# State space stage of a decoder step: gate and group norm placed in the next group's projection, one K = 2048 output product at the end

## What is computed

```python
xbc_c, conv_new = causal_conv(xbc, conv_state, p['conv_w'], p['conv_b'])     # width 4, then SiLU
xs, Bm, Cm = jnp.split(xbc_c, [D_INNER, D_INNER + SSD_GROUPS * D_STATE], axis=-1)
y, h_new = ssd_scan(xs, dt, A, Bm, Cm, ssm_state)                             # chunks of 128
y = y + p['d_skip'][:, None] * xs
y = y.reshape(b, T, D_INNER) * jax.nn.silu(z)
yg = y.reshape(b, T, SSD_GROUPS, D_INNER // SSD_GROUPS)
yg = yg * lax.rsqrt(jnp.mean(yg * yg, axis=-1, keepdims=True) + EPS)
y = yg.reshape(b, T, D_INNER) * p['norm_ssd']
...
merged = sigmoid(gate_a) * (att @ p['w_attn_out']) + sigmoid(gate_s) * (ssd_y @ p['w_ssd_out'])
```

## Time and profile before

| what | us |
|---|---|
| median of the runs (4490.77 to 4492.65) | 4491.07 |
| the profiled execution | 4487.59 |
| its span, first to last instruction | 4485.8 |
| PE busy in it | 4092.7 (91%) |
| VectorE busy | 1838.2 (41%) |
| ScalarE busy | 725.8 (16%) |
| POOL busy | 223.2 (5%) |
| mean granted TensorE clock | 0.942 of full speed |

### The profile page before, as it was taken

How to read it: one execution, slowest core, us unless ns; L and a number is a source line. 1 busy time by engine, 2 the same in 40 slices (tenths; PEclk the granted TensorE clock), 3 DMA queues, 4 the chain that set the end, 5 groups by cost and what they waited for, 6 DMA issues and landing times. The chain is left out here.

```text
span 4485.8 us, 48370 instructions
## 1 busy us (share of the span) xinstructions
PE 4092.7 (91%) x17960; PEld 2927.2 (65%) x17960; DVE 1838.2 (41%) x3624; ACT 725.8 (16%) x1421; POOL 223.2 (5%) x224
## 2 busy tenths in 40 slices
PE   7999999989977978988988978899988989999997
PEld 5888776656655555665655645566656678888664
DVE  4222220010035676586586575257861143333001
ACT  2000000010021220211311300145611010000000
POOL 0000000000000020010100201200000100000000
PEclk9999999999957989999999988899998999999999
DMA  4121221114132101101001011320022111111111
GB/s 171 76 112 76 94 96 64 45 70 169 71 78 64 36 22 57 38 16 57 33 21 57 28 32 56 100 71 19 6 82 96 65 50 47 38 47 42 69 39 57
DMA packets 98898, 277.21 MB, mean 62 GB/s; under 512 B 18473, under 2 KB 54321, under 8 KB 87073
## 3 DMA queue, kind: packets, MB, share of 16 engines
q1 hardware_dynamic: 80464, 239.13, 15.5%
q0 software_dynamic: 3200, 21.11, 1.3%
q10 hardware_dynamic: 15072, 14.82, 1.1%
HBM read 228.18 MB, written 47.00 MB: 61 GB/s over the span
## 5 line engine op out<-in xcount | busy, mean ns | idle before, releaser
L1648 PE MATMUL banks<-h,arena 128*128 128x344 f32 x1920 | 586.6, 465 | 30.9 <-DMA arena<-in_w_ssd 30.9
L472 PE MATMUL f_ps<-f_a,f_w 128*128 128x344 f32 x2112 | 611.2, 452 | 1.9 <-issue 1.9
L472 PEld LDWEIGHTS f_ps<-f_a,f_w 128*128 128x128 f32 x2112 | 401.1, 190 | 211.3 <-issue 2.3
L1648 PEld LDWEIGHTS banks<-h,arena 128*128 128x128 f32 x1920 | 368.7, 195 | 232.9 <-DMA arena<-in_w_ssd 32.7
L363 PE MATMUL f_ps<-h,f_w 128*128 128x258 f32 x1408 | 327.7, 386 | 13.0 <-ACT h L209 12.1
L363 PE MATMUL f_ps<-room 128*128 128x258 f32 x1408 | 328.3, 393 | 2.5 <-issue 1.8
L363 PE MATMUL f_ps<-h,room 128*128 128x258 f32 x1408 | 320.9, 381 | 1.1 <-DVE f_u L633 1.0
L363 PEld LDWEIGHTS f_ps<-h,f_w 128*128 128x128 f32 x1408 | 269.7, 192 | 64.5 <-issue 23.6
L363 PEld LDWEIGHTS f_ps<-room 128*128 128x128 f32 x1408 | 275.1, 196 | 45.8 <-issue 2.7
L363 PEld LDWEIGHTS f_ps<-h,room 128*128 128x128 f32 x1408 | 266.9, 190 | 41.0 <-DVE f_u L633 1.9
L707 PE MATMUL banks<-y,arena 128*128 128x344 f32 x768 | 239.2, 474 | 38.2 <-DVE y L2058 30.1
(11 more groups left out here) (380 smaller groups left out, 4866.4 us busy)
## 6 DMA issues: line engine op xcount, KB each, us to landing
f_wa<-in_w_ada SPq DMA_DIRECT2D x28, 1024.0 KB
f_w<-in_w_f1i SPq DMA_DIRECT2D x22, 1024.0 KB, 4.7
f_w<-in_w_f2i SPq DMA_DIRECT2D x22, 1024.0 KB, 4.7
arena<-in_w_ssd SPq DMA_DIRECT2D x40, 512.0 KB, 3.6
f_w<-in_w_f1o SPq DMA_DIRECT2D x16, 704.0 KB, 4.1
f_w<-in_w_f2o SPq DMA_DIRECT2D x16, 704.0 KB, 4.1
room<-in_x SPq DMA_DIRECT2D x16, 516.0 KB, 7.7
scr_x<-room SPq DMA_DIRECT2D x16, 516.0 KB, 5.2
```

The lines of the kernel that those rows point to most:

```text
L472: m = nc.tensor.matmul(ps[n][:, q, 0:NC], wo[:, hf, k], a[:, hf * OK + k, n * NC:(n + 1) * NC], start=hf == 0 and k == 0, stop=hf == 1 and ...
L1648: m = nc.tensor.matmul(ps[q][:, c, 0:NC], w[:, q, k], h[:, k, c * NC:(c + 1) * NC], start=k == 0, stop=k == KT - 1)
```

## The change

The loop over g becomes four copies in the code. ssd_out is run once, behind the last scan.

Gate, squares, sums, root and scaling of group g - 1 stand in the projection of group g, for g of 1 to 3: the gate opens VectorE's list; ScalarE's squares stand ahead of its first copies; POOL adds the four squares into one tile (the first is written there); PE sums that tile over the channels with one product for each chunk of 344, behind its third, fourth and fifth chunk; ScalarE's roots stand among the copies of the second tile; VectorE scales behind probe 0. SP stores the finished four tiles (2064 KB) to a scratch in HBM ahead of the sixth weight tile.

H moves from y to room, where S was accumulated; the wait on kept leaves the scan and stands on SP ahead of the load of H. Squares, their sum and the root lie in room as well. The probes get their own tile (above) instead of cv. The counts stand behind chunks 2, 7, 10, 12, 15, 16, 17 and 18. Six halves of top rounds stand in a projection in place of eight; the other 40 stand in the last stage.

The last stage gates group 3 itself, loads the other twelve tiles and multiplies 16 K tiles with each of eight weight tiles (1024 KB each, in xc's memory). Of the first weight tile the twelve old K tiles come first, with the sums behind each chunk, then group 3's four. ScalarE copies each product into S. S is no longer zeroed, and nothing is added into it.

```diff
@@ time_steps
-            nc.gpsimd.memset(S[:], 0.0).then_inc(zeroed, 1)
-            pool.wait_ge(zeroed, UP + 1)
@@ new helpers
+def gate_group(dve, nc, g, xc, zs, y, dskip, skip, gated):
+    for t in range(GT):
+        nc.vector.scalar_tensor_tensor(out=y[:, t], in0=xc[:, t], scalar=dskip[:, g * GT + t:g * GT + t + 1], in1=y[:, t],
+                                       op0=ALU.mult, op1=ALU.add).then_inc(skip, 1)
+        dve.wait_ge(skip, UP + t + 1)
+        nc.vector.tensor_tensor(y[:, t], y[:, t], zs[:, t], ALU.mult).then_inc(gated, 1)
+def add_group(pool, nc, acc, sq, squared, pooled):
+    for t in range(1, GT):
+        pool.wait_ge(squared, UP + t + 1)
...
+        nc.gpsimd.tensor_tensor(acc[:], acc[:], sq[:, t % 2], ALU.add).then_inc(pooled, 1)
+def sum_group(pe, nc, out, ones, acc, n, pooled, root, summed):
+    pe.wait_ge(pooled, UP + GT - 1)
+    if n:
+        pe.wait_ge(root, UP + n)
+    nc.tensor.matmul(out[0][:, 0:NC], ones[:], acc[:, n * NC:(n + 1) * NC], start=True, stop=True).then_inc(summed, 1)
...
@@ ssd_project
+        COUNT_AT = {2: 0, 7: 1, 10: 2, 12: 3, 15: 4, 16: 5, 17: 6, 18: 7}
...
+                    if g:
+                        sp.wait_ge(kept, 16 * g)
+                    sp.dma_start(H.rearrange("p q b n -> p (q b n)"), d["state_ssm"][g]).then_inc(H_in, 16)
                 if t >= 2:
                     sp.wait_ge(mm, UP + NCH * (t - 1))
+                if t == 5 and g:
+                    sp.wait_ge(scaled, UP + GT * NCH)
+                    sp.dma_start(scr["ys"][g - 1], y[:]).then_inc(y_out, 16)
                 sp.dma_start(w[:, t % 2], d["w_ssd"][g][t]).then_inc(w_in[t % 2], 16)
...
-                    if done % 2 == 1 and done // 2 < PROBES:
-                        count_rows(done // 2)
+                    if g and 2 <= done < 2 + NCH:
+                        sum_group(pe, nc, pU, ones, acc, done - 2, pooled, root, summed)
+                    if done in COUNT_AT:
+                        count_rows(COUNT_AT[done])
...
+            if g:
+                square_group(act, nc, y, acc, sq, gated, pooled, squared)
+            copy(0)
+            for c in range(NCH):
+                if g:
+                    root_group(act, nc, pU, rstd, eps, c, eps_set, summed, root)
+                copy(1, (c,))
...
+                gate_group(dve, nc, g - 1, xc, zs, y, dskip, skip, gated)
             dve.wait_ge(pad, UP + 1)
-            probes(range(5))
+            probes(0)
+            if g:
+                scale_group(dve, nc, g - 1, y, rstd, nssd, gated, root, inv, scaled)
+            probes(1)
             convolve(0)
-            dve.wait_ge(act_done, UP + 2)
-            probes(range(5, PROBES))
+            probes(2, 3)
             convolve(1)
+            probes(4, 5, 6, 7)
@@ ssd_scan
-            act.wait_ge(kept, 16 * (g + 1))
@@ ssd_out
+            for j in range(g):
+                n = min(GT, OLD - 2 - GT * j)
+                sp.dma_start(olds[:, GT * j:GT * j + n], scr["ys"][j][:, 0:n]).then_inc(old_in[j], 16)
+            sp.wait_ge(gated, UP + GT)
+            sp.dma_start(w[:, 0], d["w_so"][0]).then_inc(w_in[0], 16)
+            sp.dma_start(zs[:, 0:2], scr["ys"][g - 1][:, GT - 2:GT]).then_inc(old_in[g - 1], 16)
...
+                for ks in (range(OLD), range(OLD, KS)) if t == 0 else (range(KS),):
...
+                    nc.scalar.activation(S[:, t, c * NC:(c + 1) * NC], ps[t % 2][:, c, 0:NC], ACT.Copy).then_inc(read[t % 2], 1)
...
-            with dve.Fori(0, KT // 2) as i:
-                top_round(dve, nc, chosen_rows(mask), m8, found, tick, 2 * len(CHOSEN) * i)
...
-                        nc.vector.tensor_tensor(part, part, ps[q][:, c, 0:NC], ALU.add).then_inc(read[q], 1)
+            top_half(dve, nc, rows, m8, found, 0)
+            scale_group(dve, nc, g, y, rstd, nssd, gated, root, inv, scaled)
+            for n in range(1, ROWS):
+                top_half(dve, nc, rows, m8, found, n)
@@ ssd_branch
-        with nc.Fori(0, SG) as g:
+        for g in range(SG):
```

More of the change, by code:

```diff
@@ L1036 @@
 PROBES = 32 // SG
+EARLY_HALVES = 6
 PROMPT_ROUNDS = SHARE - KT // 2
@@ L1553, in ssd_project @@
+def ssd_project(nc, arena, banks, start, room, d, o, scr, kept, pick, g, h, xb, xc, zs, cw, cb, y, mask, dt, dtA, ones, ident, dskip, nssd):
     R, PD = SH // SG, DI // SH
@@ L1587, in ssd_project @@
                                 "hscaled", "mmu", "upd"))
+        eps_set, skip, gated, squared, pooled, summed, root, inv, scaled, y_out = (
+            ph.sem(n) for n in ("eps_set", "skip", "gated", "squared", "pooled", "summed", "root", "inv", "scaled", "y_out"))
         block = ph.block()
@@ new lines, in _ @@
+            for t in range(2, KT):
+                sp.wait_ge(mm, UP + NCH * (t - 1))
+                sp.dma_start(w[:, t % 2], d["w_so"][t]).then_inc(w_in[t % 2], 16)
+        @block.gpsimd
+        def _(pool):
+            add_group(pool, nc, acc, sq, squared, pooled)
+        @block.tensor
+        def _(pe):
+            for t in range(KT):
+                q = t % 2
+                pe.wait_ge(w_in[q], UP + 16 * (t // 2 + 1))
+                if t >= 2:
+                    pe.wait_ge(read[q], UP + NCH * (t // 2))
+                for ks in (range(OLD), range(OLD, KS)) if t == 0 else (range(KS),):
+                    for c in range(NCH):
+                        if t == 0 and ks[0] == 0:
+                            for j in range(g):
+                                pe.wait_ge(old_in[j], UP + (32 if j == g - 1 else 16))
+                        elif t == 0:
+                            pe.wait_ge(scaled, UP + GT * (c + 1))
+                        for k in ks:
+                            m = nc.tensor.matmul(ps[q][:, c, 0:NC], w[:, q, k], tiles[k][:, c * NC:(c + 1) * NC],
+                                                 start=k == 0, stop=k == KS - 1)
+                        if ks[-1] == KS - 1:
+                            m.then_inc(mm, 1)
+                        else:
+                            sum_group(pe, nc, pU, ones, acc, c, pooled, root, summed)
@@ L2033, in _ @@
-        @block.tensor
-        def _(pe):
-            for t in range(GT):
-                pe.wait_ge(squared, UP + t + 1)
-                for n in range(NCH):
-                    m = nc.tensor.matmul(ps[1][:, n, 0:NC], ones[:], sq[:, t % 2, n * NC:(n + 1) * NC],
-                                         start=t == 0, stop=t == GT - 1)
-                m.then_inc(summed, 1)
-            project_tiles(pe, nc, w, ps, y, w_in, mm, read, KT, kt=GT, made=(scaled, GT))
+            square_group(act, nc, y, acc, sq, gated, pooled, squared)
```

146 lines of the change are left out of this document (84 added, 62 removed).

## The result

The changed kernel takes 4375.09 us, the median of four runs (4372.62 to 4380.48), beside 4491.55 of the kernel before: a ratio of 0.9742 with a 95% interval of 0.9725 to 0.9759. Two further measurements gave 0.9746 [0.9733, 0.9759] and 0.9746 [0.9732, 0.9759].

A forecast was written before the change was run, and what follows sets the result against it. TensorE idles in the serial gate-and-norm chain between scan and next projection. Output stages -259.5, projections -7.4 and -15.2, semaphores +1.8, last stage +176.3 give -104.0; 4487.6 - 104.0 + 3.5 = 4387 us, range 4376 to 4418.

The forecast's parts named there:

- A: Projections of groups 1 to 3: PE waits at its first sum and the sixth tile; 30 us, 4417; chance 0.17.
- B: Last stage: loads take 36.3 us or VectorE's halves run over; +9 to +16, about 4400; chance 0.08.
- C: Each projection: PE waits for the finished norm, not only the sum; some 17 us three times, 4438; chance 0.04.
- D: Last stage: TensorE's clock stays at 1.2 GHz after idling some 30 us; 224 us more, 4611; chance 0.03.
- The cover at the sums: Projections of groups 1 to 3: POOL's third add done at 18.3 us, PE asks at 19.7; 1.4 to spare.
- The step that failed: Last stage, from the scan's end: 3.2 + 27.1 + 232.3 = 262.6 us against 86.3 before, +176.3.
- the carry to the median: From profiled execution to median of runs: +3.5 us, taken from the kernel before.
- The load: Last stage: all 7216 KB needed before PE's first matmul, 27.1 us; bounds 22.6 to 36.3.
- VectorE's 39 halves: Last stage, behind the scaling: 19 maxima at 5.01 and 20 replacements at 5.35, 202.2 us, ending at S + 232.3.
- Stage change behind a projection: End of each projection: ten more semaphores to clear at 0.045 us each, four times, +1.8 us.
- The zeroing of S: On POOL, ahead of the projections: its removal priced at 0, as it stood beside longer work.
- The count's 7.4 per projection: Group 0's projection: own probe tile and later counts remove PE's wait for ScalarE's silu, -7.4 us; similarly in later groups.

The follow-up runs named there:

- the longer load: The changed kernel with the first group's stored tiles loaded a second time in the last stage (2064 KB more): 4383.03 us, ratio 0.9760.

## Why the prediction was off, point by point

**Right in kind.** The signs that the prediction had named came in kind: shorter projections (by 8.3 and by 5.3 to 6.2), no idle time over 2 us at the sums or at the sixth tile, 7.3, 9.5 and 6.8 (7.1) from a scan's end to the next projection, a last stage whose first matmul waits for its load, 24.6 behind the scan (30), and VectorE ending last there, 1.24 behind ScalarE (2.4). A (gate not covered), B (a longer last stage), C (not overlapped) and D (clock) didn't come. The cover at the sums is 2.3 in group 1 where 1.4 was forecast (1.5 to 4.4 over the groups of three profiles), and the doubled adds show that it is real: 4.3 more on POOL's third signal (22.2 for 17.9) turned into waits of 1.1 to 2.0. The Trainium skill (SBUF — State Buffer, section "Who interferes with whom"), which the forecast weighed, is borne out by these rows: 3.40 for a product that takes 1.23 alone, and POOL's 3.17 for 2.36.

**D, the clock.** Ahead of the last product TensorE idled 25.25 us, and the granted clock was 0.50 there, its level of 1.2 GHz. In the first 8.6 us of work it was 0.68, then 1.00, 2.4 GHz, for the remaining 220.7. The price was 8.75 for twenty records in place of 5.95: 2.8, where 2.0 stood in the sum.

**The step that failed is the last stage, 262.6 by the forecast and 253.3 to 253.9 in three profiles.** It is the largest of the terms that were off, and it failed in two of its own. How much of the number it makes is below: other terms took part of it back, and the carry to the median added more.

- *The load, 27.1 from its issue to the first matmul; measured 21.8, 21.7 and 21.8* (the other 0.4 of the 5.7 is a stage change of 2.8 for 3.2). I had scaled one row, 4128 KB in 15.5, by size; that row stands in the queue behind two weight tiles, issued 0.9 ahead of it (3463.56 and 3464.42), and shares its 15.5 with them. In the windows of 2 us from 3466 to 3476 the kernel before already had 330 to 561 GB/s. And the lower bound, 22.6, was no bound: it took the 358 GB/s of the earlier trace rows for the best that the queue does, and while it streams here it does 355 to 462. The Trainium skill (DMA: Bandwidth & Descriptors, "Specifications") has 358 as the limit of a core's HBM traffic, and the forecast cited that line alone. The Trainium skill (the same page, section "Measured (HBM→SBUF, 128 partitions, SWDGE, issued from GpSimd)") has 425 for 16 MB on one core whose neighbour is idle. This case, one core at 416 over 12 us with loads issued from SP, lies near the second. Besides, the load is not one transfer: its first part is in when the gate is done, and the gate, at 14.4, sets when the rest may start.
- *VectorE's 39 halves, 202.2; measured 198.8 (2372.07 to 2570.85).* The six maxima themselves take 4.86 in the earlier trace rows and 4.86 here; what is shorter is the step behind them, 5.01 to the replacement there and 4.89 here, and 5.29 in place of 5.35 from a replacement on. The row comes from a loop on the device, in which VectorE raises a counter of its own ahead of each half (tick, in top_round); the step was still 5.00 there when only the outer loop was written out. The changed kernel's last stage is straight code without that counter; which of the two makes the step was not tried. 19 x 4.89 + 20 x 5.29 = 198.7. With the start of the halves 0.4 later than forecast (S + 30.5 for S + 30.1) this makes S + 229.3 in place of S + 232.3.

**Smaller terms, which nearly cancel.** Projection of group 0: 154.4 for 155.3, as not even the seventh count was late; groups 1 to 3: 156.5 in the mean for 157.1; in all 2.7 sooner. Stage change behind a projection: with ten further semaphores it is 1.05 longer (3.61 to 4.66 on ScalarE), not 0.45, and TensorE's way to the scan's first product grew by 1.05, 1.06, 1.4 and 1.4; together 4.9 for 1.8. The forecast's 0.045 for one came from the ends of two different stages, 3.2 read on SP and 3.6 on ScalarE. The scans of groups 1 to 3 take 57.6 in place of 56.9, 2.0 in all, where 0 was priced. They go with the clock: over their first 12 us it was granted at 0.77, 0.80 and 0.76, and at 0.85 in group 0's, which takes 56.95; with POOL's adds doubled the same three scans have 0.86 and take 56.8. Why it falls differently stays open. Scan's end to next projection: 7.3, 9.5 and 6.8 in the first profile, 2.2 over, and 21.3 in the second as forecast. Sum for the first profile: -5.7 - 3.0 - 2.7 + 3.1 + 2.0 + 2.2 = -4.1 against the forecast's -104.0, where -107.7 was measured, 3.7 beyond it.

**A term priced at nothing.** The zeroing of S "stood beside longer work: 0" in the forecast. It held VectorE up in the time steps, 2.83 for 0.31, and without it the projections start 2.0 sooner. The rows resemble the meeting of POOL and VectorE that the forecast had weighed in the gate, here on an operation with one input from SBUF; the zeroing was not taken out by itself, but all four profiles that have it show the 2.6 to 2.8, and all nine without it the 0.31.

**The bounds, and the carry to the median.** The forecast for the profiled execution was 4383.6, and it took 4380.5: 3.1 of the 12.0 us between 4387.1 and the median 4375.1. The other 8.9 are the carry: +3.5 in the forecast, and the median lies 5.4 under the profiled execution. So the largest part of the number's miss is no mechanism of the kernel. The range's lower end had a load of 22.6 and nothing for quicker halves, and it left out that one profiled execution is a sample: those of before lie 3 to 4 under their medians (with the loop written out 1.3 over), those of after 5.4 over, 0.2 under and 1.0 over theirs. Carrying +3.5 from one kernel to the other gave the median a precision that it hadn't; 5 us to either side belonged into the range.

**The term that was right by its company.** The count's 7.4 per projection looked like the price of one wait. Alone it gives 1.7. In group 0 of the changed kernel the whole is 8.3: 2.0 by the order, 2.1 by the two halves fewer, and 4.3 that came with the rest of the change, most likely with the loop written out, which frees VectorE too and alone gave nothing. The forecast had all of them and so about the right sum, but that was luck in the case of the loop, priced at 0, and a reader who took the order alone would have lost three quarters.

## What to carry to other kernels

When a stage is moved off the path, what is left on it decides the gain: here a wait of 22 us for a load and 7 us between two stages, which came down to 8 and 3, for another 28 us, by loading into memory that happens to be idle and by consuming the load in pieces. A load's price is read from the windows while its queue streams, part by part with what permits each part, not by scaling a row of another queue. The step between two instructions is not the instruction's duration: it depends on what else the engine's list holds there, and is read from a list like the new one. And edits that free the same engine have to be priced together: one that is worth nothing alone can carry another.

## What was not expected of the hardware

- One core's loads from HBM streamed at 416 GB/s over 12 us, up to 462 in single windows of 1 us (495 in the longer load); the forecast had taken the 358 of the earlier trace rows for the most that they do.
- One semaphore more in a stage made its end 0.07 to 0.11 us dearer, ten made it 1.05 dearer (3.61 to 4.66 on ScalarE).
- The exclusion between VectorE and POOL acts in both directions, on operations of either form with two inputs from SBUF: POOL's add took 3.17 behind a VectorE product, VectorE's product 3.40 behind an add, and one of two columns 1.86 for 0.15. An operation with one such input was held too, by POOL's zeroing: 2.83 for 0.31.
- Written out, the loop saved VectorE its gaps of 0.16 between dependent operations of the convolution and, alone, the kernel no time at all (ratio 0.9997).
